# Second output projection and feed-forward entry of a two-block transformer kernel, reordered

## The reference, cut to what matters

```python
h = h + rmsnorm(mix @ w_o, post_mix_norm)
hn = rmsnorm(h, pre_ffn_norm)
ff = (silu(hn @ w_gate) * (hn @ w_up)) @ w_down          # width 2816
h = h + rmsnorm(ff, post_ffn_norm)
e = rmsnorm(p @ w_ple_proj, ple_norm)
h = h + e * sigmoid(h @ w_ple_gate + b_ple_gate)
```

## Time and profile before

| what | value |
|---|---|
| three runs | 2053.14 us median (2052.69 to 2055.45) |
| the profiled execution, its own time | 2049.3 us |
| its span on the core | 2047.4 us |
| PE, DVE, ACT, POOL busy | 94%, 65%, 46%, 39% of the span |
| PE busy from 1200 to 1250, 1250 to 1300, 1300 to 1400 us | 43.39, 43.08, 86.19 us |
| PE busy from 1900 to 1950, 1950 to 2000 us | 43.34, 39.85 us |
| mean granted clock of PE | 0.985 |
| first matmul of the kernel; projection 14 of out2 | starts at 7.55 us; 1200.95 to 1206.67 us |

### The profile page before, as it was taken

How to read it: one execution, slowest core, us unless ns; L and a number is a source line. 1 busy time by engine, 2 the same in 40 slices (tenths; PEclk the granted TensorE clock), 3 DMA queues, 4 the chain that set the end, 5 groups by cost and what they waited for, 6 DMA issues and landing times.

```text
span 2047.4 us, 25425 instructions
## 1 busy us (share of the span) xinstructions
PE 1923.1 (94%) x9431; PEld 1592.8 (78%) x9431; DVE 1321.1 (65%) x1923; ACT 932.3 (46%) x1683; POOL 797.8 (39%) x565
## 2 busy tenths in 40 slices
PE   8999989998999999989997988899999999999888
PEld 8987867776878888867776776678888887877667
DVE  5376488887785443476666366876655568878835
ACT  4131269886432223256666445433333333435541
POOL 1333269994000000025664001799999950000030
PEclk9999999999999999999999989899999999999999
DMA  5111100003224111100000424132323348694202
GB/s 197 32 34 47 65 1 1 1 1 113 86 62 152 42 32 42 43 21 32 21 21 34 153 64 172 41 103 95 121 73 104 112 139 320 215 313 159 98 21 103
DMA packets 68666, 178.49 MB, mean 87 GB/s; under 512 B 6528, under 2 KB 9856, under 8 KB 68544
## 3 DMA queue, kind: packets, MB, share of 16 engines
q1 hardware_dynamic: 45744, 125.72, 18.2%
q10 hardware_dynamic: 22800, 51.15, 7.0%
HBM read 146.95 MB, written 29.88 MB: 86 GB/s over the span
## 4 chain that ended last, share of the span: by engine, by line
PE 65%; DVE 15%; ACT 5%; issue 5%; POOL 5%; DMA 4%; SPq 0%; ACTq 0%; DVEq 0%; POOLq 0%
PE psb L358 15%; PE psa L358 12%; PE psa L2597 5%; PE psc L2597 4%; DMA wr<-slabs 4%; PE psb L2597 3%; PE psd L2597 3%; PE psd L358 2%; PE psd L1059 2%; PE psc L1037 2%; PE psd L2036 2%; POOL pb L1206 1%; PE psc L2003 1%; DVE wrf L2459 1%; DVE wl L384 1%
## 5 line engine op out<-in xcount | busy, mean ns | idle before, releaser
L2459 POOL TENSOR_TENSOR wrf<-wr 128x512 f32<-128x512 f32 x100 | 164.1, 1641 | 171.0 <-DMA wr<-slabs 163.1
L1979 POOL TENSOR_TENSOR lps<-lps,tiny 128x128 f32<-128x128 f32 (+2 forms) x24 | 14.7, 614 | 467.5 <-DVE tiny L1974 467.2
L2472 ACT ACTIVATE wrh<-wrf 128x512 fp32r<-128x512 f32 x155 | 97.8, 631 | 171.4 <-DVE wrf L2459 95.1
L2477 POOL TENSOR_TENSOR wrl<-wrf,wrh 128x512 fp32r<-128x512 f32 x100 | 150.6, 1514 | 8.4 <-ACT wrh L2472 8.3
L1206 POOL TENSOR_TENSOR pb<-pb,tiny 128x1024 f32<-128x1024 f32 x64 | 121.2, 1894 | 51.9 <-DVE tiny L1165 50.1
L3216 POOL TENSOR_TENSOR esum<-esum,e 128x1024 f32<-128x1024 f32 x7 | 18.6, 2658 | 290.0 <-ACT e L3123 289.1
L384 DVE TENSOR_TENSOR wl<-wraw,wh 128x1024 fp32r<-128x1024 f32 x73 | 89.9, 1232 | 63.8 <-ACT wh L378 60.0
L358 PE MATMUL psb<-mh,wh 128*128 128x512 f32 x352 | 124.4, 398 | 4.2 <-issue 2.5
L358 PE MATMUL psb<-ml,wh 128*128 128x512 f32 x352 | 122.6, 393 | 0.0
L358 PE MATMUL psb<-mh,wl 128*128 128x512 f32 x352 | 122.2, 392 | 0.0
L378 ACT ACTIVATE wh<-wraw 128x1024 fp32r<-128x1024 f32 x80 | 84.1, 1053 | 79.6 <-PE psb L358 41.1
(11 more groups left out here) (685 smaller groups left out, 5906.6 us busy)
## 6 DMA issues: line engine op xcount, KB each, us to landing
wraw<-slabs SPq DMA_DIRECT2D x98, 512.0 KB, 3.5
wr<-slabs SPq DMA_DIRECT2D x132, 256.0 KB, 4.0
wr<-slabs SPq DMA_DIRECT2D x40, 512.0 KB, 3.6
hidden<-hf ACTq DMA_DIRECT2D x22, 512.0 KB, 3.8
half_sums<-hsum ACTq DMA_DIRECT2D x22, 256.0 KB, 3.6
x<-xT SPq DMA_DIRECT2D x8, 520.0 KB, 8.1
h<-xT SPq DMA_DIRECT2D x8, 512.0 KB, 6.4
residual<-h ACTq DMA_DIRECT2D x8, 512.0 KB, 6.7
```

The costliest lines, as they stand in the source:

```text
L2459: e.tensor_tensor(WRF[n % NW][:, :], x, y, WEIGHTS[product(n)][2]).then_inc(*done.up(("sum", n)))
L2472: e.activation(WRH[n % NW][:, :], x, ACT.Copy).then_inc(*acted.up(("high part", n)))
L2477: e.tensor_tensor(WRL[n % NW][:, :], x, WRH[n % NW][:, :], SUB).then_inc(*pooled.up(("low", n)))
```

## The change

- **Out2.** DVE splits the next slab before it adds the squares. `pe_h2_sums(0)` stands after projection 15 and not after 14, and `pe_h2_spread(0)` between the blocks of the first feed-forward projection; `act_h2_root` and `dve_h2_rstd` follow.
- **First weight blocks.** SP loads the first four blocks of `wr` at slab S_OUT2 + 10 (`sync_first_blocks`). For that SQ8 moves from 140 to 156 kB and the places of the eight unit weights change. The sums of units 0 and 1 wait for the sums of half 0, those of units 2 to 5 for the sums of half 1. ACT makes the high parts of units 0 and 1 at n = 12 and 13.
- **Spill.** The eight spills of H are issued by ACT after each `act_n3(m, 1)`, and not by SP.
- **Entry.** DVE splits slabs S_FFN + 2 to 5 one tile later in its order. ACT's and DVE's orders in `act_ffn` and `dve_ffn` change: high(2), copy of the spread and split of S_FFN + 7 stand ahead of four scaled inputs, and `x_highs(7)` follows unit 2 and not unit 5.
- **Constant products.** PE gets products of ones: 8 at the very start, 4 ahead of unit 8 and 6 ahead of unit 10.
- **Attention.** `dve_four(7)` stands at u = 2, `dve_norms(0)` at u = 1; the meta scores of g = 1 wait for `four(7)`; PSB moves by 0.25 kB.
- **End.** The sum of squares of EB (7 additions of 128 x 1024) is DVE's and not POOL's. `e sums` and `e spread` stand one projection earlier, the slabs S_PLEG + 4 and 5 are split two projections earlier in DVE's order, `act_h3` stands one step later than before behind the copies to EB, S_PLEG is split two tiles earlier, and GH 7, GL 6 and GL 7 have places of their own.

The core of the diff:

```diff
...
         QSB = at("qsb", [P, NL], F32, 203.5)
-        PSB = at("psb", [P, NL], F32, 162.5)
+        PSB = at("psb", [P, NL], F32, 162.75)
...
         PTL = [at(f"ptl{j}", [P, 8, HALF], F32R, (43, 84.25)[j]) for j in range(2)]
...
         O2 = at("o2", [P, KT, T], F32, 172)
-        SQ8 = at("sq8", [P, 8, HALF], F32, 140)
+        SQ8 = at("sq8", [P, 8, HALF], F32, 156)
         ACC3 = at("acc3", [P, T], F32, 132)
...
         TH = at("th", [P, T], F32, 188)
...
         WR = at("wr", [P, NR, 1024], F32, 140)
-        _at = (156, 160, 164, 168, 124, 128, 132, 136)
+        _at = (124, 128, 156, 160, 164, 168, 132, 136)
         WRH = [at(f"wrh{j}", [P, HALF], F32R, _at[j]) for j in range(NW)]
...
         WRF = [at(f"wrf{j}", [P, HALF], F32, _at[j] + 2) for j in range(NW)]
...
         OB = [at(f"ob{j}", [P, T], F32, 172 + 4 * j) for j in range(4)]
-        GH = [at(f"gh{m}", [P, T], F32R, 43 + 4 * m if m < 7 else 27) for m in range(KT)]
-        GL = [at(f"gl{m}", [P, T], F32R, (124, 128, 132, 136, 109, 113, 31, 35)[m]) for m in range(KT)]
+        GH = [[at(f"gh{m}{h}", [P, HALF], F32R, 43 + 4 * m + 2 * h if m < 7 else (117, 27)[h]) for h in range(2)]
+              for m in range(KT)]
+        GL = [at(f"gl{m}", [P, T], F32R, (124, 128, 132, 136, 109, 113, 87, 119)[m]) for m in range(KT)]
         PS = [ctx.enter_context(nc.psum_tensor(f"ps{n}", [P, 2, HALF], F32)) for n in "abcd"]
...
         MUL, ADD, SUB, MAX = ALU.mult, ALU.add, ALU.subtract, ALU.max
...
                 t.then_inc(*(psum.up(name, ("used", s)) if used else psum.up(name)))
+
+        def constant_products(e, out, n):
+
+            for _ in range(n):
+                e.matmul(out[:, 0:256], lhsT=ONE[:, 0:1].to_broadcast([P, P]),
+                         rhs=ONE[:, 0:1].to_broadcast([P, 256]), start=True, stop=True, skip_group_check=True)
...
                 e.wait_ge(*vec.on(("meta s", g - 1)))
+            if g == 1:
+                e.wait_ge(*vec.on(("four", 7)))
             for v in range(4):
...
                 t = e.matmul(PS[Dp][:, 0, 2 * v * META:2 * v * META + 2 * META].rearrange("p (a b) -> p a b", b=META),
...
                     dve_maxima(e, u)
-                if 0 < u - 1 < NU:
+                if 0 <= u - 1 < NU:
                     dve_norms(e, u - 1)
-                if u == 0:
-                    dve_norms(e, 0)
+                if u == 2:
                     dve_four(e, 7)
...
                     dve_outputs(e, g - 1)
...
                     pe_o2_spread(e, 0)
-                if n == 14:
-                    pe_h2_sums(e, 0)
-                if n == 15:
-                    pe_h2_spread(e, 0)
+            pe_h2_sums(e, 0)
...
                     act_n3(e, m, 0)
-                if n == 14:
-                    act_h2_root(e, 0)
+                if n in (12, 13):
+                    act_high(e, n - 12)
+            act_h2_root(e, 0)
             act_o2_root(e, 1)
...
                 act_n3(e, m, 1)
+                load(e, f"spill2{m}", hs2[m], H[:, m, :])
                 if m == 1:
...
                 if m % 2:
...
                 h, m = divmod(n, 8)
+                dve_split(e, S_OUT2 + n + 2)
                 e.wait_ge(*acted.on(("o2 sq", n)))
...
                     e.tensor_tensor(half(ACC3, h), half(ACC3, h), half(RS2, n % 2), ADD).then_inc(*vec.up(("acc3", n)))
-                dve_split(e, S_OUT2 + n + 2)
                 if n == 8:
...
                 for m in FIRST_HALF.get(n, ()):
...
                     dve_pair(e, KT - 2, 0)
-                if n == 14:
-                    dve_h2_rstd(e, 0)
+            dve_h2_rstd(e, 0)
             dve_o2_rstd(e, 1)
...
                 dve_h2(e, m, 1)
-                if m % 2:
-                    dve_split(e, S_FFN + 2 + m // 2)
+                if m and m % 2 == 0:
+                    dve_split(e, S_FFN + 1 + m // 2)
             dve_n3(e, KT - 1, 1)
             dve_pair(e, KT - 2, 1)
+            dve_split(e, S_FFN + 5)
             dve_h2_rstd(e, 1)
...
-        def sync_spill(e):
-            for m in range(KT):
-                e.wait_ge(*vec.on(("h2", m, 0)))
-                e.wait_ge(*vec.on(("h2", m, 1)))
-                load(e, f"spill2{m}", hs2[m], H[:, m, :])
+        def sync_first_blocks(e):
+            e.wait_ge(*vec.on(("mix2", "low", LATE[-1], 1)))
+            for x in (1, 3, 0, 2):
+                e.dma_start(WR[:, x, :], slabs[S_GATE_UP + x]).then_inc(*blocks[x].up(("slab", x)))
         def sync_blocks(e):
-            e.wait_ge(*psum.on(("h2 sums", KT - 2, 1)))
-            for x in (1, 3, 0, 2, *range(4, 4 * (NCK - 1))):
-                if x >= NR:
-                    e.wait_ge(*low_done(last_unit(x - NR)))
+            for x in range(NR, 4 * (NCK - 1)):
+                e.wait_ge(*low_done(last_unit(x - NR)))
                 e.dma_start(WR[:, x % NR, :], slabs[S_GATE_UP + x]).then_inc(*blocks[x % NR].up(("slab", x)))
...
                 p, kt = UNITS[n]
...
                     e.wait_ge(*psum.on(("o2 sums", 1)))
+                elif n >= 2:
+                    e.wait_ge(*psum.on(("h2 sums", KT - 2, 1)))
+                else:
+                    e.wait_ge(*psum.on(("o2 sums", 0)))
                 x, y = weight_blocks(n)
...
                                                     7: lambda: pe_h2_sum(e, 4, 1)} if h else
-                            {3: lambda: pe_o2_sums(e, 1), 6: lambda: pe_o2_spread(e, 1)})
+                            {3: lambda: pe_o2_sums(e, 1), 4: lambda: pe_h2_spread(e, 0), 6: lambda: pe_o2_spread(e, 1)})
                     if h == 1 and j == 0:
...
                     if h == 1 and j == 1:
...
                     e.wait_ge(*vec.on(("scaled" if p == 2 else "hidden", 0, w)))
+                if w == 0 and p in (7, 3):
+                    constant_products(e, up_bank(w, 3), 4 if p == 7 else 6)
                 if p not in (2, 5):
...
             elif p == 1:
...
                 act_scaled_input(e, kt + 4)
-            act_high(e, 0)
+            act_high(e, 2)
+            act_h2_copy(e, 1)
+            act_split(e, S_FFN + 7)
             act_scaled_input(e, 2)
             act_scaled_input(e, 6)
-            act_h2_copy(e, 1)
-            act_high(e, 1)
-            act_split(e, S_FFN + 7)
-            act_high(e, 2)
+            act_high(e, 3)
             act_scaled_input(e, 3)
             act_scaled_input(e, 7)
-            act_high(e, 3)
+            act_high(e, 4)
+            act_x_highs(e, 1)
             act_tanh(e, 0, 0)
-            act_x_highs(e, 1)
-            act_high(e, 4)
+            act_high(e, 5)
             act_tanh(e, 0, 1)
-            act_high(e, 5)
             act_high(e, 6)
...
             for n in range(NUP):
...
                 act_high(e, n + 7)
-                if c == 1 and w in (5, 6, 7):
-                    act_x_highs(e, {5: 7, 6: 3, 7: 4}[w])
+                if c == 1 and w in (2, 6, 7):
+                    act_x_highs(e, {2: 7, 6: 3, 7: 4}[w])
                 if w == (11 if c == 1 else 3) and c != 2:
...
                 if c == 1 and w == 13:
...
         def dve_ffn(e):
-            dve_x_sums(e, 1, range(3))
+            dve_x_sums(e, 1, range(2))
             dve_split(e, S_FFN + 7)
+            dve_x_sums(e, 1, range(2, 4))
             dve_scaled(e, 0, 0)
-            dve_x_sums(e, 1, range(3, 4))
             dve_scaled(e, 0, 1)
+            dve_x_lows(e, 1)
             dve_gated(e, 0, 0)
             dve_hidden(e, 0, 0)
-            dve_x_lows(e, 1)
             dve_gated(e, 0, 1)
...
             dve_x_sums(e, 6)
...
                     e.wait_ge(*acted.on(("ple gate", m - 3, h)))
-                project(e, S_PLEG + m, full, lambda kt, c, n: GH[kt][:, c:c + n], lambda kt, c, n: GL[kt][:, c:c + n],
+                project(e, S_PLEG + m, full, lambda kt, c, n: GH[kt][c // HALF][:, 0:n], lambda kt, c, n: GL[kt][:, c:c + n],
                         [(PS[m % 3][:, h, :], h * HALF, HALF)], ("ple gate", m, h),
                         hi=lambda kt: acted.on(("h3 high", kt, h)), lo=lambda kt: vec.on(("h3 low", kt, h)), used=h == 1)
+                if n == 5:
+                    e.wait_ge(*vec.on(("e sum", KT - 1)))
+                    token_sums(e, Dp, ESUM, SQC[:, 1, 0:1], 1, "e sums")
                 if n == 6:
-                    e.wait_ge(*pooled.on(("e sum", KT - 1)))
-                    token_sums(e, Dp, ESUM, SQC[:, 1, 0:1], 1, "e sums")
-                if n == 7:
                     e.wait_ge(*vec.on("e rstd"))
...
                     act_f_root(e, 1)
-                act_h3(e, m, 0)
+                if m:
+                    act_h3(e, m - 1, 0)
+            act_h3(e, KT - 1, 0)
             act_split(e, S_PLEG + 1)
...
                 act_h3(e, m, 1)
...
             if m >= 3:
-                e.wait_ge(*pooled.on(("e sum", m - 2)))
+                e.wait_ge(*vec.on(("e sum", m - 2)))
             e.wait_ge(*acted.on(("eb", m)))
...
             e.wait_ge(*vec.on(("h3", m, h)))
-            if m == KT - 1 and h == 0:
```

(37 more changed lines are left out.)

## The result

The changed kernel takes 2021.57 us (median of 4 runs, 2019.01 to 2024.49) against 2052.91 for the kernel before: ratio 0.983, 95% interval 0.9809 to 0.9852, 31.3 us saved. Forecast were 2009 us and 43.9 us saved. The profiled execution took 2019.83 us with a span of 2017.7.

A forecast was written before the change was run, and what follows sets the result against it. PE, busy 94% of the span, was taken as the bound; gains 12.9 + 15 + 2.6 + 13 + 0.4 = 43.9 us off the 2053.1 median gave 2009 us; forecast range 2004 to 2014 (0.62), eight in ten 2000 to 2026.

The forecast's parts named there:

- rival B: Behind half 0's sums, meta scores, unit 10, gate projection 2: new gaps lower the clock, 2.3 us each; 2018 us, chance 0.11.
- rival A: First chunk: the port lock makes DVE the bound, all 36 two-input operations at 1.70 us; 2023 us, chance 0.12.
- rival C: Chunk 2 takes back seam and chunk gains because weights of units 14 and on come late; 2025 or 2037 us, chance 0.05.
- rival D: All units: new places of the weight tiles cost PE more per unit; 2063 us at 0.25 us a unit, chance 0.03.
- First chunk: From half 1's last sum of squares to chunk 2: waits before units shrink; 15 us gained, bounds 13.5 and 18.
- Sums(3) and (4), half beside POOL, end at S + 46.6, ACT's highs and the lows that follow at S + 49.4: Ahead of unit 10: when its inputs are ready, in us after half 1's last sum of squares (S).
- with every POOL operation of the stretch beside a DVE one: First chunk's slow bound: the low parts come 3 to 4 us later, gain 13.5 us.
- Seam and entry: Out2's projection 14 to half 1's last sum of squares: gain 12.9 us, 9.3 at the seam and 3.6 behind it.
- by the burst of rows 3 without loss of clock: Behind projection 15: four sums in one 3.6 us burst keep full clock, like the profile's burst from 815 to 818.6.
- Attention: PE's 5.43 us wait for exp(1): exp(1) comes 4.4 us earlier; 2.6 us gained, bounds 0 and 4.5.
- The end: PE's gaps at `ple` step 3 and gate projections 5 and 8 shrink or go; 13 us gained, bound 10.
- Start: Eight constant products at the very start cover the slow first 4 us; 0.4 us gained, bounds -0.6 and 1.3.

The follow-up runs named there:

- e6: Changed kernel with POOL's list from unit 14's weight sum on held until DVE's low parts of product 3 are done; unit 10 came 34.35 us after unit 0, not 37.87.
- e8: Changed kernel with the first four weight blocks loaded late again and ACT's feed-forward list in its old order; unit 14 came 56.84 us after unit 0.
- e12: The changed kernel itself, run again in a second set of 5 runs; 2021.10 us, ratio 0.9831 to the kernel before.
- e7: Changed kernel with ACT's high parts of product 7 one unit earlier and DVE's sums of product 3 ahead of product 7's low parts; 2015.21 us, one run.
- e11: Changed kernel with half 0's sums of squares between the first feed-forward projection's blocks and ACT's high parts of product 7 one unit earlier; 2030.98 us, ratio 0.9878.
- e1: Kernel before with only the eight constant products ahead of the first projection; 2053.78 us, ratio 1.0002.
- e3: Kernel before with only the changes of the end; 2042.86 us, ratio 0.9946.
- e4: Kernel before with only the changes of out2, the feed-forward entry and the first chunk; 2038.52 us, ratio 0.9926.
- e5: Changed kernel without the four and six constant products ahead of units 8 and 10; run once, unit 14 came 51.47 us after unit 0 (changed 51.45).
- e2: Kernel before with only the attention part; ratio 0.9998 (0.9988 to 1.0008).

## Why the prediction was right, and where it was too high

**The direction and the places were right, the size only in part.** The time lies outside the forecast's own 2004 to 2014 us and between those of rivals B (2018) and A (2023), and two of the signs of being wrong came: a wait for `xa` above 3 us behind the constant products (5.5), and a clock near 0.5 behind the seam. Projection 15 stood directly behind 14 but for 0.6 us, the waits named went, unit 0 came 16.8 us after the last sum of squares, as replayed, and nothing was lost in chunk 2 (f - U14 shrank by 2, so rival C is out). Units run at 2.72 us as before: rival D is out. Rival B named four places for a low clock, and it came in all four: behind the sums of half 0 and at unit 10 (below), at the meta scores (0.50 from 272 to 277 us), where a low stretch had stood before too, and at gate projection 2 (0.50 from 1935 to 1940 in the changed kernel, not in e6, e8 and e12). About 32 of 43.9 us came by the stages. Of the first chunk's 15 us 8.5 came (6.8 ahead of unit 0, 1.7 behind it), of the seam's 12.9 nine, of attention and start, 3.0, nothing that is seen at O; 13 came in the end; 1.7 that were not forecast came between unit 14 and f, where single profiles of the two kinds overlap.

**First chunk: the term that was mis-sized.** Forecast from U0 to U14 were 60.3 - 16.8 = 43.5 us; it took 51.5, against 53.8 before. (S is 1256.8 in the changed kernel's profile.) The step that failed is "Sums(3) and (4), half beside POOL, end at S + 46.6, ACT's highs and the lows that follow at S + 49.4". The sums ended at S + 47.9; the low parts took 6.00 us beside POOL where 2.5 were counted, and unit 10 began at S + 54.6, then at a clock of 0.50 (2.7 us more by U14). e6 shows the 3.5 us by themselves, e7 and e11 that a closed gap of DVE comes back as slower operations or later waits, e8 that more of POOL's list beside DVE's costs 4 us and more. This is rival A's mechanism, at half its price: not every DVE operation ran at 1.70. The bound "with every POOL operation of the stretch beside a DVE one" (3 to 4 us later) was passed too, at 5. By the Trainium skill ("SBUF — State Buffer", section "SBUF: two separate sides"), which has the two engines take that port in turn, lows(7) should end near S + 41 (the prediction's estimate); they ended at 1297.56, S + 40.75. The trace agrees, though not with DVE busy all that time: 3.61 us of it DVE stood idle for ACT, which waited for a sum of POOL's, and POOL was late because its operation before took 4.22 us beside DVE. The sum above went back to 0.62 us an operation for the lows of product 3, where POOL's list still ran.

**Seam and entry, 12.9 forecast.** From O, unit 0 came at 163.6 us before (mean of before and e1 to e3) and 147.8 after (mean of the changed kernel, e4, e5 and e12): 15.8, of which 6.8 are the part from the last sum of squares, so 9.0 here. The step that failed is "by the burst of rows 3 without loss of clock". In all seven profiles with this burst (changed, e4 to e8, e12) the clock fell 2.3 to 3.0 us into it, which cost the changed kernel 1.1 us in the burst and 2.1 in the nine matmuls behind it. The row from 815 to 818.6 was one draw of fourteen: in e2, e3, e5 and e12 the clock fell in that very burst (windows of e3):

```profile
815.00:818.60 3.60, 3.60 (x29) 0.91 0.02 5
818.60:823.00 4.40, 4.40 (x22) 0.50 0.00 0
```

Where it stays low until 13 us after the burst began, unit 0 is 1.6 us later still. The rest are small waits (0.8, 0.3 and 0.2 us between the entry's projections) that the replay did not have. That the early blocks removed the 5.1 us wait was also wrong in its cause (e8): it stays away without them, by the traces because the spills no longer stand ahead of the blocks.

**Attention, 2.6 forecast, 1.7 measured at its place (e2), nothing at O.** In the changed kernel `four(7)` ended at 275.5 and not at 272.3, since two of its operations took 1.9 us each beside POOL, and PE waits 2.5 us for it. By 280 the changed kernel and before stand at the same matmul (279.99 and 280.05), although attention began 1.4 us later in the changed one.

**The end, 13 forecast:** 153.5 to 139.9 us, the mean of the ten profiles with it; with e4's 150.9 among those without it, 13 us. DVE's additions took 1.23 us each, as counted (the row that the prediction names for it, 2.58 / 2, makes 1.29). **Start, 0.4 forecast, nothing measured (e1):** the step that failed is that PE, held at DVE's last sum of squares, loses nothing more there; the wait at it (0.7 to 1.0 us near 28) had a low clock behind it in eight of ten profiles, a place that rival B doesn't name.

**The base.** The profile of before had O at 1121.7, 5 us earlier than the mean of 14 profiles (1126.6); that it lay 3.8 us below the median is of this. Making the sum of gains on it and taking it off the median was right; comparing it stretch by stretch with one trace of after was not.

## What to carry to other kernels

Compare stages from a common instruction, and profile the same code twice before a difference of a few us is given a cause. Where two engines contend for a port, count their work one after the other through to the operation that PE waits for; a gap closed in either list is otherwise paid back in longer operations. Before a burst is moved off PE's list, ask what PE would wait for in its place. And when a wait goes away, read what released it before and what is released earlier now: here, by the traces, the moved spills did what the early blocks were given credit for.
